# Weight slots of a float32r decoder kernel placed 128 bytes off their matmul partners, without per-slot shifts

## The reference

```python
def _swiglu(x, w_gate, w_up, w_down):
    return (jax.nn.silu(x @ w_gate) * (x @ w_up)) @ w_down

for l in range(DEPTH):
    x = _layer_norm(DN_ALPHA * x + 0.5 * _swiglu(x, ffn1...), ln1_g[l], ln1_b[l])
    mix = _hybrid_mixer(x, positions, w_in[l], ..., w_out[l])   # z = x @ w_in, three branches, gates, merged @ w_out
    x = _layer_norm(DN_ALPHA * x + mix, ln2_g[l], ln2_b[l])
    x = _layer_norm(DN_ALPHA * x + 0.5 * _swiglu(x, ffn2...), ln3_g[l], ln3_b[l])
```

## Time and profile before

| | us |
|---|---|
| median of 3 runs | 1305.36 (1305.18 to 1305.45) |
| the profiled execution's own time | 1305.84 |
| its span | 1303.5 |
| TensorE matmuls busy | 1291.5 (99%) |
| TensorE weight loads busy | 1167.2 (90%) |
| VectorE busy | 891.4 (68%) |
| ScalarE busy | 639.0 (49%) |
| DMA queue of the loads, share of 16 engines | 55.5% |

### The profile page before, as it was taken

The page is one execution under the profiler, slowest core; times in us unless marked ns, Lnnn a source line. Parts: engine busy times, 40 slices in busy tenths (PEclk is TensorE's granted clock), DMA queues, the critical chain, the costliest instruction groups (busy, mean ns, idle before and its releaser), DMA issues.

```text
span 1303.5 us, 18950 instructions
## 1 busy us (share of the span) xinstructions
PE 1291.5 (99%) x8173; PEld 1167.2 (90%) x8173; DVE 891.4 (68%) x1086; ACT 639.0 (49%) x654; POOL 69.4 (5%) x59
## 2 busy tenths in 40 slices
PE   8999999999999999999999999999999999999998
PEld 8888889998999998888898888899989998988886
DVE  6666667898755676555676666779987556766655
ACT  5444446585534354444454444456755434544441
POOL 0398000000000000000000000000000000000000
PEclk9999999999999999999999999999999999999999
DMA  8755656535565555566556555556345555555562
GB/s 291 235 188 185 192 183 186 180 98 167 161 190 162 195 171 185 193 194 194 164 191 194 191 186 190 173 166 194 130 130 182 175 177 178 185 187 188 188 193 95
DMA packets 176243, 234.83 MB, mean 180 GB/s; under 512 B 7904, under 2 KB 146784, under 8 KB 176032
## 3 DMA queue, kind: packets, MB, share of 16 engines
q1 hardware_dynamic: 175776, 231.78, 55.5%
q0 software_dynamic: 240, 1.71, 0.4%
q10 hardware_dynamic: 144, 0.13, 0.1%
HBM read 232.56 MB, written 1.05 MB: 179 GB/s over the span
## 4 chain that ended last, share of the span: by engine, by line
PE 98%; DVE 1%; ACT 1%; DMA 0%; DVEq 0%; issue 0%
PE ps L1461 22%; PE ps L1450 22%; PE ps L1376 11%; PE ps L1375 11%; PE ps L1374 11%; PE ps L1449 9%; PE ps L1439 5%; PE ps L1453 1%; PE ps L1396 1%; PE ps L1408 1%; PE ps L1656 1%; PE ps L1615 0%; PE ps L1616 0%; ACT rot_sw L625 0%; PE ps L1641 0%; PE ps L1643 0%
## 5 line engine op out<-in xcount | busy, mean ns | idle before, releaser
L830 DVE TENSOR_TENSOR wlo<-raw,whi 128x2048 fp32r<-128x2048 f32 (+1 forms) x218 | 491.6, 2272 | 191.8 <-ACT whi L539 191.6
L539 ACT ACTIVATE whi<-raw 128x2048 fp32r<-128x2048 f32 (+1 forms) x218 | 413.7, 1899 | 295.8 <-DMA raw<-ffn_w_gate 109.8
L1450 PE MATMUL ps<-xpair,whi 128*128 128x512 f32 x1216 | 419.0, 395 | 0.0
L1449 PE MATMUL ps<-xpair,wlo 128*128 128x256 f32 x1064 | 296.5, 279 | 0.0
L1450 PEld LDWEIGHTS ps<-xpair,whi 128*128 128x128 f32 x1216 | 220.8, 188 | 41.2
L1374 PE MATMUL ps<-xpair,whi 128*128 128x256 f32 x800 | 225.1, 281 | 0.0
L1376 PE MATMUL ps<-xpair,wlo 128*128 128x256 f32 x800 | 223.7, 280 | 0.0
L1375 PE MATMUL ps<-xpair,whi 128*128 128x256 f32 x800 | 223.3, 279 | 0.0
L1449 PEld LDWEIGHTS ps<-xpair,wlo 128*128 128x128 f32 x1064 | 199.9, 188 | 6.2
L1375 PEld LDWEIGHTS ps<-xpair,whi 128*128 128x128 f32 x800 | 149.9, 187 | 0.5
L1374 PEld LDWEIGHTS ps<-xpair,whi 128*128 128x128 f32 x800 | 149.5, 187 | 0.4
(11 more groups left out here) (234 smaller groups left out, 1685.5 us busy)
## 6 DMA issues: line engine op xcount, KB each, us to landing
raw<-w_in SPq DMA_DIRECT2D x60, 1024.0 KB, 5.2
raw<-ffn_w_down SPq DMA_DIRECT2D x44, 1024.0 KB, 4.9
raw<-ffn_w_gate SPq DMA_DIRECT2D x43, 1024.0 KB, 5.3
raw<-ffn_w_up SPq DMA_DIRECT2D x43, 1024.0 KB, 5.3
raw<-w_br SPq DMA_DIRECT2D x12, 1024.0 KB, 5.1
raw<-w_out SPq DMA_DIRECT2D x8, 1024.0 KB, 4.9
raw<-mla_w_uq SPq DMA_DIRECT2D x4, 576.0 KB, 3.9
raw<-mla_w_ukv SPq DMA_DIRECT2D x2, 1024.0 KB, 4.9
```

Of the source, the lines that this page charges most:

```text
L539: act.activation(unit(whi, n), unit(raw, n), ACT.Copy).then_inc(w_hi, 1)
L830: dve.tensor_tensor(w_low(n), unit(raw, n), unit(whi, n).bitcast(F32), ALU.subtract).then_inc(w_lo, 1)
L1449: pe.matmul(ps[:, bank, 0:SEQ], wl[:, kk, cols], xhi[:, kk, :], start=False, stop=False)
L1450: last = pe.matmul(ps[:, bank, :], wh[:, kk, cols], xpair[:, kk, :, :], start=kk == 0, stop=kk == KC - 1)
```

## The change

Two unnamed regions of up to 128 bytes (`BESIDE`) are laid ahead of the `raw` ring and between `whi` and `xpair`, and the shifts within the slots go, with the functions that computed them. `raw`, `wlo` and `whi` now begin at 64 (remainder to 256), and `xpair`, the hidden parts, latents, branches and merged parts at 192. So weights and activations are 128 bytes apart for every kind of matmul above, whichever of the two moves. The 14 loads that waited for one unit more wait as all others do. On every engine the same instructions stand in the same order as before.

```diff
@@ -31,7 +31,6 @@
 UNIT = 2048
 RING = 5
-PITCH = UNIT + 64
 U_FFN = 3 * NF
@@ -40,7 +39,7 @@
 FFN_BASE = (0, U_FFN + U_MIX)
 MIX_BASE = U_FFN
 N_UNITS = DEPTH * U_LAYER
-LINE, SHIFT = 64, 16
+LINE, BESIDE = 64, 128
@@ -127,9 +126,11 @@
-    r_raw = region(4 * RING * PITCH)
-    raw, wlo = (place(name, [P, RING * PITCH], dt, r_raw) for name, dt in (("raw", F32), ("wlo", F32R)))
-    whi = sb("whi", [P, RING * UNIT + SHIFT], F32R)
+    region(BESIDE)
+    r_raw = region(4 * RING * UNIT)
+    raw, wlo = (place(name, [P, RING, UNIT], dt, r_raw) for name, dt in (("raw", F32), ("wlo", F32R)))
+    whi = sb("whi", [P, RING, UNIT], F32R)
+    region(BESIDE)
     xpair = sb("xpair", [P, KC, 2, SEQ], F32R)
@@ -304,34 +305,9 @@
-    def shift_of(n):
-
-        k = n % U_LAYER - MIX_BASE
-        if 0 <= k < U_MIX:
-            return SHIFT if k < 2 or 16 <= k < MIX_FIXED or k >= U_MIX - MIX_OUT else 0
-        return 0 if k in (-MIX_BASE, 1 - MIX_BASE) else SHIFT
-
     def unit(ring, n, lo=0, size=None):
 
-        if ring is whi:
-            at_n = n % RING * UNIT + shift_of(n) + lo
-        else:
-            at_n = n % RING * PITCH + (0 if is_paired(n) else shift_of(n)) + lo
-        return ring[:, at_n:at_n + (size or size_of(n))]
-
-    def is_paired(n):
-
-        k = n % U_LAYER
-        k -= FFN_BASE[1] if k >= FFN_BASE[1] else 0
-        return 2 <= k < U_FFN - 1 and (k - 2) % 3 < 2
-
-    def freed_by(n):
-
-        meets_next = n % RING < RING - 1 and shift_of(n) > shift_of(n - RING + 1)
-        return n - RING + 1 if meets_next else n - RING
-
-    for n in range(1, N_UNITS):
-        assert n % RING == 0 or shift_of(n - 1) <= shift_of(n)
+        return ring[:, n % RING, lo:lo + (size or size_of(n))]
@@ -402,7 +378,7 @@
             if n >= RING:
-                sp.wait_ge(w_used, done_no(freed_by(n)))
+                sp.wait_ge(w_used, done_no(n - RING))
```

## The result

| | before | after |
|---|---|---|
| median, us | 1305.4 (1305.18 to 1305.45, 4 runs) | 1320.64 (1320.13 to 1321.24, 4 runs) |
| ratio, 95% interval | | 1.0116 [1.0104, 1.0128] |
| the profiled execution's own time, its span | 1305.84, 1303.5 | 1320.83, 1318.5 |

What follows compares the result with a forecast made beforehand. TensorE was taken as the bound, the time being the sum of spacings between matmul starts. Only the pairs counted, -7.2 us, all other terms 0: from 1305.4 to 1298.2 us, range 1284 to 1314 (the forecast's own case 1294 to 1303).

Steps and rivals of the forecast that it cites:

- steps 1 and 2: SP's 14 waits ending one unit earlier, gain 0; VectorE and ScalarE using the rings at other addresses, price 0.
- step 3: Transposes by the identity, with x, z and hid going from 0 to 192: taken as 0, under 1 us each way.
- Step 4: 1632 matmuls with moving weights, going from distance 0 to 128: taken as 0, bounds 0 to +8.8 us.
- Step 6: Pairs, going from 0 and 192 to 128: long matmul 5.9 ns shorter, 1216 times, -7.2 us; other bound +5.4 us.
- Step 5: 3132 triples, going from distance 192 to 128: taken as 0, bounds -13.8 and +1.9 us.
- D: Distance 0 was the good one for 512 columns and is left: moving weights +8.8 us, 1314.2 us; chance 0.25.
- B: 128 is the best distance for all, triples lock at 113.3 ns: -13.8 us more, 1284.4 us; chance 0.22.
- C: The distance only shifts when the streams meet, gains in one kind paid in another: 1305.4 us; chance 0.20.

## Why the prediction was wrong

The frame held. The time is the sum of TensorE's spacings, they follow the distance by kind (for triples with two states), and steps 1 and 2 cost nothing (waits put back: 1320.5; after the change the same two waits of TensorE). For step 3, all 569 matmuls of other forms, the transposes among them, came out 0.03 us shorter together. The three terms of the sum were each mis-sized, all in the same direction:

- **Step 4, moving weights, taken as 0.** Measured +4.8 ns, +7.8 us, and again +7.7 us with this kind alone. Its upper bound (+5.4 ns, +8.8 us, from the earlier trace rows) was nearly the value. I had two points, 227.5 at distance 0 and 232.9 at 192, and chose the lower for 128 without a row that spoke for it. With 0, 64, 128, 192 measured at 226.7, 228.8, 232.5, 233.3 ns, distance 0 stands out and 128 is nearly as bad as 192.
- **Step 6, pairs, taken as -7.2 us.** Measured +3.4 us, and +3.1 us alone. I looked at the slow member and gave its load a better distance: the long one gained 0.9 ns, not 5.9. The same edit took the short one's load off distance 0, and that cost 3.6 ns, 4.4 us. I had this as the other bound (+5.4 us) and dropped it. The inference "512 columns at 192 are slow, so leaving 192 helps" carried a price from a matmul with moving weights to one with moving activations, and the long one at 128 is still at 231.4 ns. The 233.4 ns that I started from was too high as well: it took the short one at the 113.3 of another kind, where the means before are 115.7 and 232.3.
- **Step 5, triples, taken as 0.** Measured +1.2 ns, +3.6 us, over its upper bound of +1.9 us. Unit 4 passes 112 and 144 among six other remainders; its mean says nothing on a unit that stays at 128. Its own 96 matmuls rose by 0.4 ns with the change, the other triples by 1.2.

**The rivals.** What happened is D with the upper bounds of pairs and triples, 1321.5 forecast and 1320.6 measured, a case that I gave about 0.12 and left outside the range. That it comes so near is partly luck: moving weights and pairs fell 1.0 and 2.0 us short of their bounds, and triples went 1.7 beyond theirs. Its reason held for moving weights and the short one, which lost by leaving 0; the long one is slow with all at 0 (233.9 ns). B (128 best for all) fell: at 128 no unit of triples ran at 113.3. C (no more than a shift) fell: the mean of moving weights changes by up to 6.1 ns between distances, and the time by 1.2%. The Trainium skill (TensorE: Matmul & The Clock Gate, "Step-by-step: what each phase is for") says that TensorE has two independent read ports into SBUF, so that loading the next weights takes no read bandwidth from the running matmul. Its ports can't be counted here, but the sum of 0 that I drew from it is not what this kernel shows: the same run of 24 with moving weights spreads over 6.6 ns a matmul (226.7 to 233.3) with addresses alone. What in the memory makes spacings depend on them no run here shows.

**The range** ended at D's 1314, which has the upper bound of moving weights alone. Pairs (+3.4) and triples (+3.6) came on top. I let the three terms vary as if apart, but one edit took all three kinds off distances that, for each kind as a whole, were better than 128, so their losses came together.

## What to carry to other kernels

Where TensorE is the bound and starts a matmul every 113 to 233 ns, the remainder to 256 bytes between the moving operand and the *next* stationary one is worth up to 6 ns per matmul, about 1% of the time here; measure it for each form of matmul, since one distance is not best for all (64 for triples, 0 for moving weights and for the `whi` of pairs). When an edit moves several operands at once, write down for every load what it leaves as well as what it gains; and when the row is missing that would price a step, and the present placement sits at the best row there is, expect a loss from moving.

## What was unexpected of the hardware

**Two locked states for one address pattern.** A stretch of triples (one unit, 48 matmuls; of the latents, 27) keeps one spacing from its second matmul to its last, and at three of the four distances two such spacings were seen. The stretches of each kernel, without unit 4 (mixed remainders), the short key parts of unit 11, and the four at the ends of the FFNs where these had another distance:

| distance of the triples | spacing of a stretch, ns, and how many |
|---|---|
| 0 (all at 0) | 119.7 to 120.0: 64 |
| 64 (all at 64) | 113.3 to 113.8: 17; 117.8: 47 |
| 128 (the change) | 118.5 to 118.8: 56; 119.9 to 120.0: 8 |
| 192 (before) | 113.3: 2; 117.8: 58 |
| 192 (moving weights at 128) | 113.3 to 113.4: 16; 117.8: 44 |

The last two rows have the same triples at the same distance. With the waits put back the change has 56 and 8 as well, but not the same ones. A stretch at the shorter spacing saves 4.5 ns for each matmul, so that 14 more of them are worth about 3 us; the kernel of the last row also had the widest runs, 1309.7 to 1312.3, which would fit states that change from execution to execution, but one trace of each kernel can't show that. In the traces of the last two rows the load of the next weights starts 3.3 to 3.4 ns after the matmul that covers it in the stretches at 113.3 or 113.4, and 2.4 to 3.1 ns after it in the others, in the mean of a stretch; which is cause and which effect they don't say. What leads to 113.3 stays open, as do distances finer than 64 bytes and other mixtures of `whi` and `wlo`, which weren't tried. Were all triples at 113.3, they would give some 15 us by an estimate (118.3 less 113.3, times 3036), far more than the best placement found.
